# The readout of a state-space scan: four column tiles of the array in turn, instead of one after the other

## The reference

```
bu_re = einsum('bsgh,gph->bsgp', ug, b_re)      # and bu_im, times a coefficient per state
x_re, x_im = scan over the tokens of  x = ab * x + bu   (complex, one decay per state)
y = einsum('bsgp,ghp->bsgh', x_re, c_re) - einsum('bsgp,ghp->bsgh', x_im, c_im)   # times a factor
y = y + d_skip * u
```

## Time and profile before

| | |
|---|---|
| median of 3 runs | 3883.69 us |
| the profiled execution's own time | 3876.75 us |
| its span | 3875.1 us |
| TensorE busy, share of the span | 95% |
| VectorE, ScalarE | 67%, 55% |
| granted TensorE clock, mean over the span | 0.975 |

### The profile page before, as it was taken

The page is one execution under the profiler, slowest core; times in us unless marked ns, Lnnn a source line. Parts: engine busy times, 40 slices in busy tenths (PEclk is TensorE's granted clock), DMA queues, the critical chain, the costliest instruction groups (busy, mean ns, idle before and its releaser), DMA issues.

```text
span 3875.1 us, 76721 instructions
## 1 busy us (share of the span) xinstructions
PE 3697.2 (95%) x26662; PEld 3442.9 (89%) x26662; DVE 2601.7 (67%) x4834; ACT 2132.5 (55%) x3806; POOL 66.1 (2%) x125
## 2 busy tenths in 40 slices
PE   7999878999999999999999998999997899999998
PEld 6999748899999999887888887988997899999998
DVE  5786534568887677655577877878656566666555
ACT  3444624456666667655455555554553466666553
POOL 1000000000000000000000000000000000000000
PEclk9999868999999999999999999999998999999999
DMA  6896104555555555465788874444454455655554
GB/s 255 318 344 238 31 0 143 179 158 179 177 177 175 162 159 162 145 209 182 233 305 332 321 270 133 152 130 150 133 171 140 157 174 181 185 182 183 173 184 156
DMA packets 183869, 720.81 MB, mean 186 GB/s; under 512 B 20416, under 2 KB 22976, under 8 KB 170688
## 3 DMA queue, kind: packets, MB, share of 16 engines
q1 hardware_dynamic: 166464, 608.57, 48.6%
q0 software_dynamic: 14352, 102.77, 7.6%
q10 hardware_dynamic: 2928, 7.83, 0.6%
HBM read 714.89 MB, written 4.19 MB: 186 GB/s over the span
## 4 chain that ended last, share of the span: by engine, by line
PE 89%; DVE 6%; ACT 2%; issue 2%; DMA 0%; DVEq 0%; ACTq 0%; SPq 0%
PE PS L390 21%; PE PS L392 21%; PE PS L391 20%; PE PS L523 6%; PE PS L524 6%; PE PS L525 6%; PE PS L705 1%; PE PS L754 1%; DVE wlo L1254 1%; ACT whi L875 1%; DVE big L1322 1%; PE PS L580 1%; PE PS L647 1%; PE PS L601 0%; PE PS L417 0%
## 5 line engine op out<-in xcount | busy, mean ns | idle before, releaser
L1254 DVE TENSOR_TENSOR wlo<-raw,whi 128x512 fp32r<-128x512 f32 x2300 | 1543.3, 690 | 1034.0 <-ACT whi L875 1019.1
L875 ACT ACTIVATE whi<-raw 128x512 fp32r<-128x512 f32 x2300 | 1431.3, 630 | 1451.0 <-PE PS L392 1095.1
L390 PE MATMUL PS<-hhi,whi 128*128 128x256 f32 (+1 forms) x7104 | 2031.8, 286 | 87.7 <-DVE hlo L1267 25.8
L392 PE MATMUL PS<-hhi,wlo 128*128 128x256 f32 (+1 forms) x7104 | 2007.1, 283 | 0.0
L391 PE MATMUL PS<-hlo,whi 128*128 128x256 f32 (+1 forms) x7104 | 2006.8, 282 | 0.0
L390 PEld LDWEIGHTS PS<-hhi,whi 128*128 128x128 f32 x7104 | 1346.7, 190 | 115.1 <-issue 72.3
L392 PEld LDWEIGHTS PS<-hhi,wlo 128*128 128x128 f32 x7104 | 1347.2, 190 | 0.0
L391 PEld LDWEIGHTS PS<-hlo,whi 128*128 128x128 f32 x7104 | 1344.0, 189 | 1.0
L523 PE MATMUL PS<-whi,hhi 128*128 128x512 f32 x1024 | 404.5, 395 | 4.9 <-issue 3.5
L524 PE MATMUL PS<-wlo,hhi 128*128 128x512 f32 x1024 | 404.4, 395 | 0.0
L525 PE MATMUL PS<-whi,hlo 128*128 128x512 f32 x1024 | 404.1, 395 | 0.0
(11 more groups left out here) (400 smaller groups left out, 2206.8 us busy)
## 6 DMA issues: line engine op xcount, KB each, us to landing
raw<-peer_u_dram SPq DMA_DIRECT2D x256, 512.0 KB, 3.6
raw<-peer_v_dram SPq DMA_DIRECT2D x256, 512.0 KB, 4.3
raw<-w_in_dram SPq DMA_DIRECT2D x240, 512.0 KB, 4.2
big<-w_mod_dram POOLq DMA_DIRECT2D x96, 1024.0 KB, 5.3
raw<-w_up_dram SPq DMA_DIRECT2D x176, 512.0 KB, 3.6
raw<-w_down_dram SPq DMA_DIRECT2D x88, 512.0 KB, 3.5
raw<-w_out_dram SPq DMA_DIRECT2D x64, 512.0 KB, 3.5
raw<-w_query_dram SPq DMA_DIRECT2D x32, 512.0 KB, 3.5
```

What stands on the lines that cost most here:

```text
L390: pe.matmul(out, hi, rhi, start=start, stop=False, **more)
L392: return pe.matmul(out, lo, rhi, start=False, stop=stop, **more)
L875: f(whi[:, m % PAIRS, quarter(q)], raw[:, m % RING, quarter(q)], ACT.Copy).then_inc(hi_ready, 1)
L1254: dv.tensor_tensor(wlo[:, m % PAIRS, quarter(q)], raw[:, m % RING, quarter(q)], whi[:, m % PAIRS, quarter(q)], ALU.subtract).then_inc(lo_r ...
```

## The change

In `read_out` the two loops change places. Before, the four terms of one feature group follow one another, then the next group's; now one term of all four groups, then the next term. The operands, the places in bank 6, `start` on the first term and `stop` on the last, the two waits ahead and the one increment behind are as before. The increment hangs on the last matmul, which is term 3 of group 3 in both.

```diff
                 pe.wait_ge(s5_x, n + 1)
                 pe.wait_ge(s5_ys, n)
-                for q in range(4):
-                    for k, (part, of) in enumerate(((0, ta), (2, tb), (1, q_), (1, p))):
+                for k, (part, of) in enumerate(((0, ta), (2, tb), (1, q_), (1, p))):
+                    for q in range(4):
                         last = pe.matmul(PS[32 * q:32 * q + 32, 6, 0:SEQ], cc[:, part, 4 * n + q, :], of[:, q, :],
                                          start=k == 0, stop=k == 3)
                 last.then_inc(s5_y, 1)
```

## The result

The changed kernel takes 3854.19 us (median of 7 runs, 3853.53 to 3873.57) against 3883.31 us of the kernel before in the same comparison (7 runs, 3878.31 to 3894.14). The ratio is 0.9938, 95% interval 0.9921 to 0.9955: faster by 0.62%, 0.45 to 0.79%. Run again beside another kernel it gave 0.9936 (0.9914 to 0.9958). The forecast was 0.54%. The profiled execution took 3854.19 us with a span of 3852.6 us, 22.5 us less than before.

The account below looks back on a forecast made before the run. TensorE, busy 95% of the span, was taken as the bound; 8 calls x 2.64 us = 21.1 us, so 3876.75 - 21.1 = 3855.6 us, or 3862.6 against the median; forecast 3861, range 3850 to 3879.

Parts of the forecast that it names:

- The price of a call: Readout matmuls L754 on TensorE: a call falls from 4.52 to 1.88 us, saving 2.64 us in each of 8 calls.
- a stagger: Start delay between column tiles in a readout call: 0.01 to 0.03 us each for three tiles.
- four full streams: Readout on four column tiles at once, each reading all 128 partitions: assumed undiminished at 0.216 us a pass per tile.
- The queue: Each column tile's own queue on TensorE holds three or so waiting passes without holding up the next tile's matmuls.
- Does it arrive: Splits after each readout: VectorE's lateness, 0.4 us after the first call, dies within the step, so the saving arrives.
- Two streams: Rival: only two column tiles stream at once in a readout; 7 us saved, 3877; chance 0.13 together with three streams.
- the blocked queue: Rival: in a readout, a pass waiting for its own tile holds up all behind it; 3 us saved, 3881; chance 0.05.
- breaks at each change of tile: Rival: in a readout each tile change flushes what was loaded; 7.4 us a call, 23 us slower, 3907; chance 0.04.
- VectorE as the bound: Rival: half the saving given back as waits before L390 for VectorE's split; 10 us saved, 3873; chance 0.06.
- The chances: Whole kernel, 0.5% (19.4 us) as edge: faster 0.49, same 0.47, slower 0.04; forecast itself 0.72.

Follow-up runs that it names:

- e1: Changed kernel with terms 0 and 1 of each group, then terms 2 and 3 (four passes in a row on a tile): 1.90 us a call.
- e2: Changed kernel with terms 0, 1 and 2 of each group, then term 3 of each (six passes in a row, then two): 3.23 us a call.
- e3: Changed kernel with groups 0 and 1 in turn over all terms, then groups 2 and 3 in turn: 2.75 us a call, run 3879.54 us.
- e4: Changed kernel with all 16 matmuls of each readout issued twice: 3.59 us a call, ratio 0.9981 to the kernel before.
- e5: Changed kernel with only one of four terms read out, 4 matmuls a call instead of 16: 0.57 us a call, stretch 243.65 us.
- a1_changed: The changed kernel itself, run again beside the head-sum version: 3858.53 us, ratio 0.9936 to the kernel before.
- e6: Changed kernel with all 16 matmuls of a readout on one column tile, other groups' sums left out: 7.02 us a call.
- e7: Changed kernel with head sums also spread over four column tiles and spreading matmuls reading 128 partitions: 3845.47 us, ratio 0.9912 to the kernel before.

## Why the prediction was right

**The price of a call.** Forecast 1.88 us from 8 x 0.216 + 0.025 + 0.09 and a stagger; measured 1.86. The stagger is 7 ns a tile, below the 10 to 30 assumed. L743 was the right row to go by: it showed four tiles at work, and L754's own loads in twos showed that column tiles do the same. The step from there to four full streams was the open one, with 0.72 on it. It held without any loss: the durations are the same 379 ns.

**The queue.** "Three or so waiting passes seem to be what such a queue holds" was read from the 0.90 us between new tiles in the old order. e1, e2 and e3 were worked out from it and measured 1.90 (1.86), 3.23 (3.2) and 2.75 (2.75). That is four orders of the same work beside the old one, and e1 and e3 show besides that the places are each tile's own, which the prediction took for granted.

**Does it arrive.** Forecast: VectorE late by 0.4 us at the first split after a call and level again by the third; at the sixth call 1.3, 0.6, none. The trace has no idle time at the first two splits and 0.78 at the third after the first call; after the sixth the third split has 0.32 us of idle time before it. The waits of L390 for `wlo` moved along at 4.0 us, and the rounds take 32.82, 32.76 and 32.80 us where 32.76 was forecast. What was not foreseen lies outside the stretch: 1.3 us of the 22.5 in the profiled pair, and the larger difference of the medians.

**The rivals.** Two streams would give 3.66 us a call, the blocked queue 4.14, breaks at each change of tile 7.4; all three fall with 1.86. The rule of the Trainium skill ("TensorE: Matmul & The Clock Gate", Part 3: Packing small matmuls) that weight loads overlap matmuls in flight only where the row groups differ doesn't hold for these column tiles: all 32 loads share the rows, and they go in fours. VectorE as the bound falls with e4 and with the rounds of e5.

**The chances.** The saving was forecast at 21.1 us with the edge between "faster" and "the same" at 19.4, so which side the result would fall on was near to a toss. The measured 0.62% lies beyond the edge of 0.5%, but its interval, 0.45 to 0.79%, reaches below it: that time was saved is shown, that it was more than 0.5% is not shown by the times alone (the 21.2 us of the stretch are 0.55%). The centre of the forecast, 3861, was set near the median of before. The median after came out lower, 3854, since five of seven runs fell at 3853.5 to 3858.4; by the traces these 7 us are not the change's doing.

## What to carry to other kernels

Small matmuls on different tiles of the array run at the same time, but only as far as their order in the program lets them: on this chip a tile takes three waiting passes (of 256 fp32 columns, two to a matmul; no other width was tried), and a longer run on one tile holds up the others. So count the passes in a row on a tile in the loop order, keep them to four, and look for weight loads that go in twos or fours in the trace. Where the tile is not given by the data, as with the head sums, choose it so that neighbours in the order fall on different tiles; that was worth 5.1 us a call (7.0 to 1.9), about twice what a readout gained. Both pay in full here because TensorE leads the chain at these places; what they give where another engine leads was not measured.

## What the runs showed of the hardware that I had not expected

**Column tiles start 7 ns apart.** In the changed kernel the first matmuls of the four tiles start within 0.02 us, 7 ns from tile to tile with two passes each. In e1, with four passes each, they start within 0.04 us, 13 ns from tile to tile. That comes to 3 to 4 ns for a pass handed out, an estimate from these two. The Trainium skill ("TensorE: Matmul & The Clock Gate", Part 3: Packing small matmuls) gives about 4 ns from tile to tile for packed matmuls. That is near the figure for a single pass, and below the 7 and 13 ns between tiles here. In Part 1 of the same page the skill gives a floor of about 25 ns between two starts, and between different tiles that isn't seen here.

**The spread between runs has a place.** The same kernel ran in 3853.7 and in 3875.4 us. The profiled execution of a1_changed is one of the long ones, span 3873.8, that of the changed kernel's first comparison a short one, 3852.6. They part mostly in the first layer's attention, where TensorE works in short pieces: the last matmul of L647 starts 0.8 us later in the long run (486.8 against 486.0), the last of L580 15.4 us later (613.3 against 597.9), of 21.2 us in all. Windows of the short run:

```profile
410.00:497.00 87.00, 71.02 (x309) 58.66 (x308) 53.34 (x81) 55.94 (x61) 0.00 (x0) 0.81 0.00 1
497.00:560.00 63.00, 48.88 (x152) 28.87 (x152) 19.92 (x47) 17.40 (x52) 0.00 (x0) 0.69 0.00 0
560.00:640.00 80.00, 65.95 (x337) 52.37 (x338) 33.47 (x56) 26.93 (x53) 0.00 (x0) 0.73 0.28 94
```

and of the long one:

```profile
410.00:497.00 87.00, 71.14 (x307) 58.80 (x305) 53.20 (x81) 55.42 (x61) 0.00 (x0) 0.81 0.00 0
497.00:560.00 63.00, 54.38 (x131) 31.67 (x132) 14.59 (x34) 13.17 (x37) 0.00 (x0) 0.54 0.00 0
560.00:640.00 80.00, 60.68 (x224) 41.58 (x223) 30.75 (x56) 23.92 (x54) 0.00 (x0) 0.62 0.16 56
```

The granted clock is 0.69 against 0.54 and 0.73 against 0.62 there, and fewer matmuls get done in the same time, 152 against 131 in the second window. (The last window, with 337 against 224, also takes in more of the dense stage that follows, which the short run reaches sooner.) The clock goes between its two levels, 2.4 and 1.2 GHz, and which one a piece of this stage meets differs from run to run. That the lower clock is the reason for the longer time is read from these rows; no run was made on it. The spread is as large as the change studied. A comparison of medians of few runs can't see 0.5%; the stretch in the trace can.

**A fall of the clock costs 1.3 to 1.6 us.** After TensorE's wait of 2.5 us behind the head variance the granted clock fell to 0.50 (1.2 GHz, the lower level) for some 3 us in e2, e5, e6, e7 and a1, and stayed at 1.00 in the other five, before and after among them. The program around the wait is the same in all but e7. The profiled run of a1 is the same kernel as the changed one, and its stretch is 254.24 us against 252.67, 1.6 more. What decides it stays open: no run was made on it.
